# Score waits by head half, convolution taps, selection order and exponentials moved in a two-block transformer kernel

## The reference

```
first block, layer l:   u = rmsnorm(x);  proj = u @ w_in[l]
   q, k, v, iq, ik, iw, cB, cC, ch, g = split(proj)
   q, k, iq, ik = rope(...)
   score = sum over 4 index heads of relu(iq . ik) * iw; the best 64 keys of each token are kept
   y_attn = softmax(q . k / 8, kept keys only) @ v @ w_attn_out        (8 heads of 64)
   y_conv = (cB * conv3(cC * ch)) @ w_conv_out                         (three taps in time)
   x += (sigmoid(g0) * y_attn + sigmoid(g1) * y_conv) @ w_mix_out
   x += relu(rmsnorm(x) @ w_up)^2 @ w_down                             (hidden 4096)
second block:           two attentions (windowed with sinks; 2-D neighbourhood), then PEER:
   qh = h2 @ w_query; s1, s2 = qh . sub_keys                           (8 heads, 128 keys a side)
   v1, i1 = top16(s1); v2, i2 = top16(s2); the best 16 of the 256 sums; g = softmax of them
   x += sum over the picked experts of gelu(h . u_expert) * g * v_expert
   rmsnorm
```

## Time and profile before

| | us |
|---|---|
| median of 3 runs | 1727.77 (1727.47 to 1728.77) |
| profiled execution, its own time | 1727.02 |
| its span | 1725.7 |
| PE busy | 1700.7 (99%) |
| PE weight load busy | 1567.1 (91%) |
| DVE busy | 1328.3 (77%) |
| ACT busy | 926.5 (54%) |

### The profile page before, as it was taken

How to read it: one execution, slowest core, us unless ns; L and a number is a source line. 1 busy time by engine, 2 the same in 40 slices (tenths; PEclk the granted TensorE clock), 3 DMA queues, 4 the chain that set the end, 5 groups by cost and what they waited for, 6 DMA issues and landing times.

```text
span 1725.7 us, 33390 instructions
## 1 busy us (share of the span) xinstructions
PE 1700.7 (99%) x11670; PEld 1567.1 (91%) x11670; DVE 1328.3 (77%) x2382; ACT 926.5 (54%) x1647; POOL 63.3 (4%) x112
## 2 busy tenths in 40 slices
PE   9999999999999999999999999999999999999997
PEld 8899899989999899999889999999999988888886
DVE  7986778778976788877775999978888766666666
ACT  5454544455454544455554555577777655444553
POOL 0000001000000122100000000000000000000000
PEclk9999999999999999999999999999999999999999
DMA  6555687755445699744344555554444455555554
GB/s 233 174 187 205 209 294 270 250 174 171 159 160 168 221 329 327 238 153 140 123 167 152 173 170 179 182 171 141 141 138 144 141 191 193 194 194 194 191 192 152
DMA packets 90122, 327.30 MB, mean 190 GB/s; under 512 B 11000, under 2 KB 11176, under 8 KB 89584
## 3 DMA queue, kind: packets, MB, share of 16 engines
q1 hardware_dynamic: 79056, 286.45, 48.8%
q0 software_dynamic: 9712, 34.36, 6.0%
q10 hardware_dynamic: 1264, 5.24, 0.8%
HBM read 323.88 MB, written 6.09 MB: 191 GB/s over the span
## 4 chain that ended last, share of the span: by engine, by line
PE 80%; DVE 16%; issue 2%; ACT 1%; DMA 0%; DVEq 0%; ACTq 0%
PE bank L213 24%; PE bank L215 24%; PE bank L214 24%; DVE Z L88 6%; DVE w_lo L190 5%; PE bank L1772 3%; PE bank L284 1%; DVE yc L88 1%; PE bank L276 1%; PE bank L1313 1%; PE bank L484 1%; DVE work L88 1%; DVE rot L88 1%; DVE top L88 1%; PE bank L1264 0%
## 5 line engine op out<-in xcount | busy, mean ns | idle before, releaser
L190 DVE TENSOR_TENSOR w_lo<-raw,w_hi 128x1024 fp32r<-128x1024 f32 x544 | 658.0, 1220 | 154.1 <-ACT w_hi L185 153.3
L185 ACT ACTIVATE w_hi<-raw 128x1024 fp32r<-128x1024 f32 x544 | 572.5, 1054 | 229.2 <-PE bank L215 162.4
L213 PE MATMUL bank<-u_hi,w_hi 128*128 128x256 f32 x2400 | 686.2, 286 | 3.7 <-DVE w_lo L190 3.0
L214 PE MATMUL bank<-u_lo,w_hi 128*128 128x256 f32 x2400 | 674.7, 281 | 0.0
L215 PE MATMUL bank<-u_hi,w_lo 128*128 128x256 f32 x2400 | 674.7, 281 | 0.0
L213 PEld LDWEIGHTS bank<-u_hi,w_hi 128*128 128x128 f32 x2400 | 453.0, 189 | 12.8 <-DVE w_lo L190 4.3
L214 PEld LDWEIGHTS bank<-u_lo,w_hi 128*128 128x128 f32 x2400 | 453.2, 189 | 2.3
L215 PEld LDWEIGHTS bank<-u_hi,w_lo 128*128 128x128 f32 x2400 | 452.9, 189 | 0.0
L215 PE MATMUL bank<-w_hi,a_lo 128*128 128x512 f32 x744 | 290.6, 391 | 0.0
L214 PE MATMUL bank<-w_lo,a_hi 128*128 128x512 f32 x744 | 290.4, 390 | 0.0
L213 PE MATMUL bank<-w_hi,a_hi 128*128 128x512 f32 x744 | 289.9, 390 | 0.0
(11 more groups left out here) (286 smaller groups left out, 1710.6 us busy)
## 6 DMA issues: line engine op xcount, KB each, us to landing
raw<-stream SPq DMA_DIRECT2D x544, 512.0 KB, 3.3
gate<-w_ada POOLq DMA_DIRECT2D x48, 512.0 KB, 6.0
t_rows<-t_by_distance POOLq DMA_DIRECT2D x8, 256.0 KB, 3.1
rpb_rows<-rpb_pad POOLq DMA_DIRECT2D x8, 224.0 KB, 4.1
bias_b<-rpb_rows POOLq DMA_DIRECT2D x16, 96.0 KB, 6.3
bias_a<-t_rows POOLq DMA_DIRECT2D x1, 1536.0 KB, 13.1
x<-x_in ACTq DMA_DIRECT2D x2, 512.0 KB, 5.5
gains_b<-gains POOLq DMA_DIRECT2D x1, 1024.0 KB, 8.7
```

The lines of the kernel that those rows point to most:

```text
L185: nc.scalar.activation(w_hi[:, s, :], raw[:, s, :], ACT.Copy).then_inc(s_hi, 1)
L190: nc.vector.tensor_tensor(w_lo[:, s, :], raw[:, s, :], w_hi[:, s, :].bitcast(F32), ALU.subtract).then_inc(s_split, 1)
L213: M.matmul(o, lh, rh, start=start, stop=False, skip_group_check=True)
L214: M.matmul(o, lh, rl, start=False, stop=False, skip_group_check=True)
```

## The change

Four edits. (1) The scores of a pair wait only for the half of q and k that they read. (2) The four taps of the convolution, which stood in pairs beside the first piece of each half of cB, are spread over four steps: tap 0 stands ahead of the second cB piece of f = 0, tap 1 and the product with bank 4 ahead of the first piece of f = 2, tap 2 ahead of its second piece, tap 3 and the product with bank 5 ahead of the second gate piece. (3) In the selection loop the first step of `select` stands ahead of the first split of the turn, and a gelu of one column stands ahead of everything on ScalarE. (4) Behind the loop the exponentials stand behind the gelu of the first piece, and the transposes of the picks are put one step later.

```diff
-                PE.wait(*marks)
+                PE.wait(*marks[hp // 2])
...
+                def taps(ff):
+                    m = VE.go((got["prod"], cw_m), V.tensor_scalar, yc[:, ff, :], prod[:, ff, 0:T], cw[:, ff, 0:1],
+                              None, ALU.mult)
+                    for j in range(1, TAPS):
+                        m = VE.go((m,), V.scalar_tensor_tensor, yc[:, ff, :], prod[:, ff, j:j + T],
+                                  cw[:, ff, j:j + 1], yc[:, ff, :], ALU.mult, ALU.add)
+                    got["taps"] = VE.go((m,), V.tensor_tensor, yc[:, ff, :], yc[:, ff, :], R, ALU.mult)
+                def times_cb(f, b, m):
+                    dst = yc[:, f:f + 2, :].rearrange("p a n -> p (a n)")
+                    m = VE.go((got["taps"], m), V.tensor_tensor, dst, dst, bank[b][:, :], ALU.mult)
+                    free[b] = (m,)
+                    y_marks.append(m)
                 for f in (0, 2):
...
-                    for ff in (f, f + 1):
-                        (the two taps)
                     yield
+                    taps(f)
                     m2 = piece_b([bank[b][:, T:2 * T]], *U)
-                    (the product with the bank)
                     yield
+                    if f == 0:
+                        taps(1)
+                        times_cb(0, b, m2)
...  (gate pieces, behind the first yield)
+                    if f == 0:
+                        taps(3)
+                        times_cb(2, 5, m2)
...
-                ready = [got[n, f, "r"] for n in "qk" for f in (0, 2)] + [got["v"]]
+                ready = [[got[n, 0, "r"] for n in "qk"], [got[n, 2, "r"] for n in "qk"] + [got["v"]]]
...  (expert_up)
-            run(exponentials)
             nc.scalar.wait_ge(*m)
             nc.scalar.activation(Z[...], bank[4 + q][:, 0:T], ACT.Gelu_apprx_tanh).then_inc(s_z, 1)
+            run(exponentials)
...  (turn of the selection loop)
+            nc.scalar.activation(c_tmp[:, 0, 0:1], one[:, :], ACT.Gelu_apprx_tanh)
-            weave(ups(), select(h), 2)
+            chosen = select(h)
+            next(chosen)
+            weave(ups(), chosen, 2)
...  (weigh, ahead of the transposes)
+            yield
             yield
```

## The result

The changed kernel takes 1718.91 us (median of 5 runs, 1718.66 to 1718.94); beside it the kernel before took 1727.47 (5 runs, 1727.39 to 1728.77). The ratio is 0.9946 [0.9935, 0.9956], so 8.56 us are gone. The forecast was 1720.0, 1.1 above it.

The account below looks back on a forecast made before the run. TensorE was taken as the bound, with only its waits winnable. Terms 3.7 + 2.4 + 0.7 + 1.0 = 7.8 us off 1727.02 gave 1719.2, for the median 1720.0; range 1717.0 to 1724.2.

Parts of the forecast that it names:

- What bounds the kernel: Whole kernel: TensorE is busy 1700.7 of 1725.7 us, so only what delays its next matmul can be won.
- Edit 1: Attention scores: released by q's first half they start without a wait; VectorE's taps decide how much is kept.
- The three sizes: Attention: waits for q of 2.14 us in layer 0 and 2.60 in layer 1, plus 1.53 of half clock.
- slot reckoning: VectorE's attention queue, timed slot by slot in the new order, to say when banks 4, 5 and the probabilities' copy are ready.
- by itself 6.27: Attention scores waiting only for their half: worth 2.14 + 2.60 + 1.53 = 6.27 us by itself.
- Edit 2: Attention with taps spread: 2.4 us won in layer 0, 3.7 in layer 1, new waits for banks 4 and 5.
- Edit 3: Selection loop: VectorE sets the 23.30 us turn; only its idle time in the first two turns is recovered, 0.7 won.
- Edit 4: Behind the loop: two waits go, 0.6 us is lost again at the first maps, 1.0 won.
- the count of `sel` at 1137.3: Behind the loop: `sel` ready at 1137.3 (before about 1137.0), its copies behind one more split.
- The clock and new waits eat half: Rival: new bank waits or a neighbour bring back the half clock, loop and exponentials give nothing; 4.6 won, 1723.2, chance 0.27.
- VectorE bounds these stretches: Rival: TensorE only waits elsewhere, just VectorE's idle 0.56 and 1.34 us in attention is won; 1725.9, chance 0.09.
- Slower by the loop: Rival: the fifth split of each loop turn, 1.34 us later, is paid in all eight turns; 1731.4, chance 0.04.

Follow-up runs that it names:

- edits 3 and 4: Two runs on the kernel before: only the selection-loop change, 1726.99 us; only the exponentials behind the gelu and the picks' transposes a step later, 1727.88 us.
- edit 2: The kernel before with only the taps spread over four steps, all scores still waiting for both halves: 1725.04 us, ratio 0.9985.

## Why the prediction was right

**What bounds the kernel.** Right: busy times stand, waits went.

**Edit 1.** The three sizes were read off right (2.05 and 2.51 in layers 0 and 1, by piece starts, against 2.14 and 2.60; the clock 1.52 against 1.53), and so was the sentence that the taps decide how much is kept. VectorE did not run quite "without a pause": its 1.27 ahead of `prod` in layer 1 is in the prediction's own rows, and its slot reckoning uses it. The prediction's "by itself 6.27" was wrong as the worth of the edit alone, which won nothing (median 1.7 above before): L484's copy is the next thing late, TensorE waits 2.3 there in each layer instead of 0.9, and these waits bring the half rate back.

**Edit 2.** The slot reckoning held. Layer 0: 2.4 predicted, 2.4 by the pieces; bank 5 was to be free for TensorE at 103.0, and the piece started at 102.91. Layer 1: 3.7 predicted, 3.8 measured. L484's wait was to fall to 0.1 and is gone. Of the new waits that for bank 4 in layer 1 came out smaller (0.52 for 0.86), those for bank 5 as reckoned (0.70 and 0.56 for 0.6), all by what taking them away gave back. One part of the difference at bank 4 is the release, put at 0.16: the product with bank 4 ended at 465.25 and the piece started at 465.31, 0.06 later. Bank 4 in layer 0, free 0.35 late by the reckoning (94.1 against 93.75), cost 0.1.

**Edit 3.** 0.7 predicted, 0.9 measured, for the reason given: idle time of VectorE in the first two turns, recovered once. Turns remain 23.3. TensorE's wait of 0.50 ahead of the first piece of a turn became three, 0.10, 0.17 and 0.23: the same sum, as VectorE's work fixes it. The first two stand at the fourth and the fifth split, for which the prediction had reckoned time to spare (0.5 at the fifth). It had none; as the sum is fixed, that cost nothing.

**Edit 4.** Here a term was mis-sized: 1.0 predicted, 1.4 measured (-2.34, +0.49, +0.09, +0.38). Both waits went, and the one at the maps came, but at 0.4 where I had 0.6. The step at fault is the count of `sel` at 1137.3, "whose copies now come behind one more split". They stand directly behind the same pair of splits as before, so nothing is added: `sel` ended at 1130.56 in the changed trace (copies 1129.48, three in 1.08), and the whole stream of VectorE was 6.22 earlier where the loop begins, which makes it 1136.8 in the prediction's frame, 0.5 sooner than reckoned. VectorE's lead at the loop's end, put at 1.25, was 1.46. The warning of the Trainium skill, page "ScalarE: Activation LUTs", section "What ACT_TABLE_LOAD costs", by which the edit would lose 1.1, did not come true: load 1.28, next activation 0.01 to 0.02 behind it, at both loads.

**The sum.** 7.8 predicted; 2.4 + 3.8 + 0.9 + 1.4 = 8.5 by the rounded steps, 8.4 by the piece starts, 8.3 in span, 8.56 in medians. The last digit of the medians means little: the kernel before is not one number. The stretches at half rate come in some executions and not in others, behind the waits of 2.0 in layer 0, 2.4 in layer 1 and 1.0 at L484, and the profiled execution of before has one of them. The prediction treated the clock as one event in layer 1; it is a chance at several places. That the execution it was read from had one such stretch, and not two as the traces of edits 3 and 4, is luck, worth 1.5. And the forecast started from 1727.77, where the five runs beside the change had 1727.47: 0.3 of the 1.1 by which it was too high.

**The range.** The low end of layer 1 is given as 2.2, but 3.7 less the 1.2 that the text allows is 2.5. The range that was taken doesn't hang on it.

**Rivals.** "The clock and new waits eat half" had the new waits about right (the longest 0.7), but the clock didn't fall behind any of them; the shortest idle time that half rate followed in these traces was 1.0. "VectorE bounds these stretches" is what happens to edit 1 alone. "Slower by the loop" fell: no idle time of VectorE in any turn.

**Open.** Why the clock fell behind one idle time and not behind another of the same length: the runs don't show it. It fell behind one or other of the waits on q, of 2.0 and 2.4, in six of eight cases, behind both of 2.3 at L484, behind two of eight of 0.8 to 1.0 there, and behind none of the five of 1.6 ahead of the picks' transposes. The waits in attention are all followed by small matmuls; whether these are needed beside the idle time wasn't tried. Nor is it shown that edit 3 wins in the time itself: alone its interval reaches from 0.9982 to 1.0001.

## What to carry to other kernels

Two waits on one queue are one problem: when the first goes, ask what the waiting engine will want next and whether the releaser can have it by then. Here the first edit alone won nothing, the second alone won 2.9, and both won 6 to 7. A new order on a full engine won only its idle time, once; for every turn to be shorter, work had to leave the engine. The engine that takes it must not get it in front of something that another one waits for at the entry, and the one that gave it away may wait for it there. And where the clock can fall behind an idle time, close the gap even with work that nobody reads: that alone gave 2.3 us here, with nine of ten runs within 1.5.

## What the runs showed of the hardware

Granted clock 0.50 for some 3 us, 1.5 us lost, came behind idle times of TensorE of 1.0, 2.0, 2.3 and 2.4 us, in the middle of a kernel that is otherwise 99% busy; once (edit 2, layer 1) it lasted some 7 us and cost 2.8. Behind idle times of 1.0, 2.0 and 2.4 in other traces, and of 1.6 ahead of the picks' transposes in five, it didn't come. It makes groups of run times for the same kernel (edit 2: 1723.5 to 1725.2 with a mean granted clock of 0.997 to 0.999, and 1727.8 to 1728.2 with 0.995).

An ACT_TABLE_LOAD between two activations cost 1.28 and 0.01 to 0.02, and a copy or a scaling (`ACT.Copy`) ran between gelus without a load. The version with taps on ScalarE has six more instructions there (1653 for 1647), the six taps and no load.
